# Weights of the seven products 64 bytes further on in their ring

## The reference, cut to what matters

```
D_MODEL = 1024
D_FF = 4 * D_MODEL

def sq_relu_mlp(h, w_up, w_down):
    return jnp.square(jax.nn.relu(h @ w_up)) @ w_down

        h2 = modulate(rmsnorm(x, norm2_g[l]), sh2, sc2)
        x = x + g2 * sq_relu_mlp(h2, w_up[l], w_down[l])
```

## Time and profile before

| | |
|---|---|
| median of 3 runs | 1684.21 us (1683.75 to 1687.3) |
| profiled execution | 1685.23 us |
| its span | 1683.4 us |
| PE busy | 1624.3 us (96%) |
| DVE busy | 1269.6 us (75%) |
| ACT busy | 921.3 us (55%) |
| POOL busy | 255.3 us (15%) |
| chain that ended last | PE 87%, DVE 6%, ACT 3%, DMA 3% |
| granted TensorE clock, mean | 0.987 |

### The profile page before, as it was taken

How to read it: one execution, slowest core, us unless ns; L and a number is a source line. 1 busy time by engine, 2 the same in 40 slices (tenths; PEclk the granted TensorE clock), 3 DMA queues, 4 the chain that set the end, 5 groups by cost and what they waited for, 6 DMA issues and landing times.

```text
span 1683.4 us, 20485 instructions
## 1 busy us (share of the span) xinstructions
PE 1624.3 (96%) x8376; PEld 1332.3 (79%) x8376; DVE 1269.6 (75%) x1457; ACT 921.3 (55%) x1070; POOL 255.3 (15%) x176
## 2 busy tenths in 40 slices
PE   6999999999999999999999999999999999999994
PEld 3768876657988989898888677888888888888883
DVE  6554876777667847474799974589999999999994
ACT  6433235443443625252633234588888887888884
POOL 0000021000028333310000100102112122121200
PEclk9999999999999999999999999899999999999997
DMA  9206821003222313131222111399999999999993
GB/s 381 81 4 242 301 90 76 0 0 126 76 100 76 127 74 129 72 134 67 79 98 76 38 39 56 131 380 414 374 386 369 378 369 369 364 378 363 383 361 115
DMA packets 54484, 322.92 MB, mean 192 GB/s; under 512 B 12529, under 2 KB 13041, under 8 KB 17778
## 3 DMA queue, kind: packets, MB, share of 16 engines
q1 hardware_dynamic: 42192, 304.76, 47.3%
q0 software_dynamic: 9216, 8.43, 2.2%
q10 hardware_dynamic: 2978, 8.37, 1.3%
HBM read 323.60 MB, written 23.07 MB: 206 GB/s over the span
## 4 chain that ended last, share of the span: by engine, by line
PE 87%; DVE 6%; ACT 3%; DMA 3%; issue 1%; POOL 0%; SPq 0%; ACTq 0%; POOLq 0%; DVEq 0%
PE ps L584 25%; PE ps L1460 20%; PE ps L1487 10%; PE ps L1088 7%; PE ps L774 3%; PE ps L750 2%; PE ps L1020 2%; PE ps L1344 2%; DVE scr L2511 2%; PE ps L1444 2%; PE ps L808 1%; ACT whi L1538 1%; DVE wlo L2201 1%; DMA xT<-in_x 1%; PE ps L880 1%
## 5 line engine op out<-in xcount | busy, mean ns | idle before, releaser
L2201 DVE TENSOR_TENSOR wlo<-raw,whi 128x2048 fp32r<-128x2048 f32 x256 | 583.8, 2302 | 129.1 <-ACT whi L1538 129.0
L1538 ACT ACTIVATE whi<-raw 128x2048 fp32r<-128x2048 f32 x256 | 485.7, 1911 | 155.1 <-PE ps L584 40.9
L1460 PE MATMUL ps<-whi,xH 128*128 128x512 f32 x512 | 203.0, 396 | 0.0
L1460 PE MATMUL ps<-whi,xL 128*128 128x512 f32 x512 | 200.3, 391 | 0.0
L1460 PE MATMUL ps<-wlo,xH 128*128 128x512 f32 x512 | 199.6, 390 | 0.0
L584 PE MATMUL ps<-hH,whi 128*128 128x512 f32 x352 | 138.8, 394 | 0.3 <-ACT dmax L2014 0.3
L584 PE MATMUL ps<-hH,wlo 128*128 128x512 f32 x352 | 137.2, 390 | 0.0
L584 PE MATMUL ps<-hL,whi 128*128 128x512 f32 x352 | 137.1, 389 | 0.0
L3242 POOL DMA_INDIRECT sum_scratch<-yb,idt x32 | 51.1, 1596 | 451.2 <-ACT yb L2141 416.9
L1460 PEld LDWEIGHTS ps<-whi,xL 128*128 128x128 f32 x512 | 96.2, 188 | 20.8
L1460 PEld LDWEIGHTS ps<-wlo,xH 128*128 128x128 f32 x512 | 96.4, 188 | 19.2
(11 more groups left out here) (517 smaller groups left out, 3542.0 us busy)
## 6 DMA issues: line engine op xcount, KB each, us to landing
raw<-in_experts SPq DMA_DIRECT2D x192, 1024.0 KB, 7.7
raw<-in_streamed SPq DMA_DIRECT2D x92, 1024.0 KB, 4.8
xT<-in_x SPq DMA_DIRECT2D x1, 2048.0 KB, 17.3
h_scratch<-hN ACTq DMA_DIRECT2D x4, 512.0 KB, 2.6
sum_scratch<-xN ACTq DMA_DIRECT2D x1, 2048.0 KB, 13.3
out<-Y SPq DMA_DIRECT2D x4, 512.0 KB, 2.7
ctxT<-in_ctx SPq DMA_DIRECT2D x1, 1024.0 KB, 20.1
Y<-sum_scratch SPq DMA_DIRECT2D x2, 512.0 KB, 5.9
```

The source lines that it names most:

```text
L1460: ins = e.matmul(b.t[:, :], l, w, start=(kk == 0 and i == 0), stop=(kk == 7 and i == 2))
L1538: e.activation(u.hi, u.raw, ACT.Copy).then_inc(*p.inc("hi", n, on="hi"))
L2201: e.tensor_tensor(u.lo, u.raw, u.hi.bitcast(F32), ALU.subtract).then_inc(*p.inc("lo", n, on="lo"))
```

## The change

The blocks of the seven products start 16 elements (64 bytes) later than the places that they share. So block 3, 7 or 11 reaches 64 bytes into what lies behind it. For that, a block's copy waits also for the ordinary halves in the place behind it, a down unit's halves wait also for the block in front of their place, and the tiles behind block 11 (`UH`, `UL`, `TH`, `TL`) move by 128 elements (512 bytes).

```
+    BLOCK = 16
...
             for j in range(7):
                 b = (first + j) % 12
-                hi = at("bhi", O_HL + 1024 * b, [4, 128], FR)
-                u.blocks.append((hi, at("blo", O_HL + 1024 * b + 512, [4, 128], FR), block_user[b]))
+                o = O_HL + BLOCK + 1024 * b
+                before = [block_user[b]]
+                if b % 4 == 3 and b < 11 and block_user[b + 1][1] == "use":
+                    before.append(block_user[b + 1])
+                u.blocks.append((at("bhi", o, [4, 128], FR), at("blo", o + 512, [4, 128], FR), before))
                 block_user[b] = ("pe", "block", i, j)
...
             b0 = (units[i].half_off - O_HL) // 1024
-            units[i].half_keys = sorted({block_user[b0 + j] for j in range(4)})
+            units[i].half_keys = sorted({block_user[b0 + j] for j in range(4)} |
+                                        ({block_user[b0 - 1]} if b0 and block_user[b0 - 1][1] == "block" else set()))
             block_user.update({b0 + j: ("pe", "use", i) for j in range(4)})
...
-    UH, UL = at("UH", PH, [8, 512], FR), at("UL", PH + 4096, [8, 512], FR)
-    TH = [at("TH", PH + 8192 + 2048 * i, [4, 256], FR) for i in range(4)]
-    TL = [at("TL", PH + 9216 + 2048 * i, [4, 256], FR) for i in range(4)]
+    UH, UL = at("UH", PH + 128, [8, 512], FR), at("UL", PH + 4224, [8, 512], FR)
+    TH = [at("TH", PH + 8320 + 2048 * i, [4, 256], FR) for i in range(4)]
+    TL = [at("TL", PH + 9344 + 2048 * i, [4, 256], FR) for i in range(4)]
...
                 p.wait_ge(*(done("pool", BLOCKS[j], n) if j in (1, 2, 3, 6) else done("dma", "u", n)))
-                p.wait_ge(*done(*before))
+                for key in before:
+                    p.wait_ge(*done(*key))
                 copy(hi, block_source(n, j), p.inc("high", n, j))
```

## The result

The changed kernel takes 1699.71 us (median of 5 runs, 1695.74 to 1702.66) against 1684.21 us (5 runs, 1682.19 to 1687.3): ratio 1.0087, 95% interval 1.0075 to 1.0098, so 12.6 to 16.5 us slower. The prediction was 1699.9. The profiled execution took 1698.21 us with a span of 1696.3; before it was 1685.23 and 1683.4. In the new kernel the products stand at line 1093 (1088 before), the down projection by k at 779 (774), the other matmuls of the block at 589 (584), whi at 1543 (1538), wlo at 2207 (2201), UL at 2694 (2688).

What follows compares the result with a forecast made beforehand. PE bounds the kernel, through its 0.120 us product step and anything delaying the seam. Two events 14.7 us, clock 1.0 and step 0 sum to +15.7 us, giving 1699.9 us against a median of 1684.21; range 1691 to 1705.

Steps and rivals of the forecast that it cites:

- First stall: Seams of chunks 2 and 3: the down projection's whi waits for PE's last product, then wlo; PE idles 4.7 us.
- Second stall: Some 8 us after each seam, PE waits at k=6 for UL of pair 3, queued behind whi: 2.6 us.
- The clock: PE's granted clock falls to half in the seam stalls: 0.5 us per event, 1.0 together, bounds 0 and 3.5.
- event: All the late whi costs at one seam, in chunks 2 and 3: 7.3 us each, 4.7 plus 2.6, without the clock.
- The step: Time between the 1008 product matmuls' starts, 0.120 us: change taken as 0, within -7 to +5 us.
- 336 matmuls still in 40.3 us: Sign of a right forecast: each chunk's product matmuls keep their 0.120 us step.
- the first rival: Waits as forecast, product step shorter, 118 to 113 ns (-2 to -7 us): 1692.9 to 1697.9 us; chance 0.27.
- The other end, 113 ns or -7: Shortest step allowed for the 1008 product matmuls: 113 ns instead of 120, giving back 7 us.
- The rule of two read ports: PE reads moving operand and weights through separate ports, so the weights' start can't matter: sum would be the waits alone.
- Back-to-back issue gap: Skill page's N/2.4 + 2.5, 109.2 ns per product matmul: the change could at most give back 10.9 us.
- Blocks' waits, UH, UL, TH, TL, ACT and DVE writes: 0: Four block copies' added waits stay covered by some 7 us; 512-byte tile moves and engine writes cost nothing: 0.
- The total: Whole kernel: two events 14.7 us plus clock 1.0, +15.7 us, to 1699.9 us.

Runs made afterwards that it cites:

- the table: Small kernel of TensorE alone, weights 0 to 448 bytes off the moving operand: steps 226.7 to 234.4 ns for 512 columns, 117.2 to 120.0 for 256.
- the mixed layouts: Kernel before, without added waits: only TH and TL 448 bytes further on, 1682.11 us (0.9982); or only hH and hL 64 bytes earlier, 1691.55 us (1.0042).
- the small kernel: TensorE alone, block and experts left out; 256-column matmuls at 64 bytes entered in different ways, also behind idles: settled steps 117.8 or 113.3 ns.

## Why the prediction was right, point by point

- **First stall.** Right in place, mechanism and size. whi starts 0.27 us behind the point at which PE would have gone on (662.75, with the products' end at 662.64 less the 0.16 that the working used), wlo ends 4.23 us on, for which I had 4.25. PE follows within 0.05 us of that and not 0.2: 4.55 us late where I had 4.7. Both chunks have it, chunk 1 has not.
- **Second stall.** The queue behind whi ran as worked out: UL of pair 3 starts at 676.37; I had 677.12 with the seam 0.53 later, so 676.6. k=6 comes 0.3 us earlier than computed. But of the 2.6 us idle only 0.80 is there in chunk 2, and in chunk 3 no wait is listed; the working had named 1 to 3 us as its sign. What filled the rest is the low clock: PE was slow instead of idle.
- **The clock.** It fell at both seams, as I took from the earlier trace rows. Its cost, 0.5 us for each event, was mis-sized in this kernel: it added nothing, because PE was slow within the time in which it would have waited, and k=6 started with UL at both seams. An event is 7.12 us, against 7.3 + 0.5. The run with the later whi shows the same low clock uncovered, 1.9 us.
- **The step.** This is the term that failed, and with it the sign "336 matmuls still in 40.3 us". I took 0 within -7 to +5, on the strength of the spread of the earlier trace rows and the fact that they have the products' shape. But those rows sit on one raster, so they couldn't speak for 64 bytes. They are also only the form of TH with bhi, and durations instead of steps, though the steps of the other forms are 120.0 too. The rows off the raster couldn't decide it either: the 113 ns there are the three matmuls on wifs, which have 36 columns of weights, so the offset wasn't the only difference. It was -3 x 0.73 = -2.2 us, the first rival, near its 118 ns end. The other end, 113 ns or -7, exists too and was had with another way in.
- **The rule of two read ports.** The Trainium skill ("TensorE: Matmul & The Clock Gate", Part 2) says that loading the next weights takes no read bandwidth from the running matmul. That the start of the weights then can't matter was my inference; the page doesn't say it. The runs refute the inference: 117.2 to 120.0 ns for 256 columns and 226.7 to 234.4 for 512, by nothing but the offset between the two operands, and at 64 bytes 113.3 with another way in. The gap of 109.2 ns a step that the same page of the Trainium skill gives ("Back-to-back issue gap") was never reached; the nearest was 113.3. The page gives this gap for an isolated matmul, without the time of its weight load, and I had left that out.
- **Blocks' waits, UH, UL, TH, TL, ACT and DVE writes: 0.** Right as far as the trace tells: PE's waits shown above have none for a block, and with the blocks back on the raster the step is 120.0 again though UH, UL, TH and TL stay moved.
- **The total.** The terms as measured make +12.0 us, my sum was +15.7 (2 x 7.3 is 14.6 and not 14.7, a slip of 0.1). 2.2 of the difference is the step, 1.4 to 1.5 the events. The medians differ by 15.5 (12.6 to 16.5), so that the forecast of 1699.9 came within 0.2 us is luck. Two things lie between 12.0 and the medians. The profiled execution started its products 0.9 late, and it stands 1.5 below the median of its kernel, while the one of before stands 1.0 above; 12.0 + 0.9 + 1.5 + 1.0 = 15.4. What the last two terms are is open, since only one execution of each kernel was traced. The other four executions of the changed kernel had a mean granted clock of 0.981 to 0.985, the profiled ones 0.985 after and 0.987 before, so part of it may be more time at the low clock, at the seams or elsewhere.

Open is what in TensorE makes the patterns. No run looked into it; the table only bars a simple rule, since 128 bytes leave the mean step of 256 columns at 120.0 and lengthen that of 512 from 226.7 to 232.1. Nor do the runs say why the mixed layouts settle at 113 to 115 ns for one half of the forms and 118 to 120 for the other.

## What to carry to other kernels

When tiles of one ring are shifted against each other, every tile's end reaches into its neighbour's place: list which copy now waits for whom, and what is queued behind it, for here 64 bytes of overlap cost 14 us and their use brought 2. Before a shift is priced at nothing because a row has no spread, ask whether that row ever had another offset. And try both, the layout and the order of places: with the same 64 bytes, another order and a useless matmul the kernel was 0.4% faster than before.

## What the hardware showed that I had not expected

- In these traces the step of back-to-back fp32r matmuls depends on the start of the weights relative to that of the moving operand, and repeats after 256 bytes: 226.7 ns at 0 and 233.3 at 64 bytes for 512 columns, 120.0 and 117.8 for 256 columns. One offset can be good for one width and bad for the other.
- At 64 bytes, 256 columns have two steady patterns, 117.8 and 113.3 ns. One to six small matmuls ahead pick one or the other, and it then holds: in the kernel for 336 matmuls (38.09 us).
- With an idle time of PE of 4.4 us at each of two seams, the granted clock was at half for 3.4 us at one and for 6.8 us at the other in the same run, and it fell before PE went on. Around idle times of 0.30, 0.51 and 1.15 us in the small kernel it stayed at 1.00.
